# Keys kept by blocks of 128, residue by residue, in a one-core hybrid decoder layer

## The chip, the cores and the metric

The program runs on one core of a Trainium2 chip. The metric is the device time of one execution in microseconds (us).

## The reference

One layer of a decoder trunk, for a prompt of 2048 tokens and for 8 decode rows. Of its four branches two matter here, both banded attention over k and v that the layer's own projection makes. Branch B has 6 heads of 64 and mixes three dilations:

```python
DIL_CONFIGS = ((128, 1), (512, 4), (2048, 16))
def _fold(a, d):          # tokens of one residue mod d become a row of their own
    n, l, h, dh = a.shape
    return a.reshape(n, l // d, d, h, dh).transpose(0, 2, 1, 3, 4).reshape(n * d, l // d, h, dh)
for window, d in DIL_CONFIGS:
    o, lse = _band_attention(_fold(q, d)[:, :, :, None], _fold(k, d), _fold(v, d), slopes[:, None], d)
```

In `_band_attention` each block of 128 queries sees its own 128 keys and the 128 before them, with a bias of -slope * distance. At dilation 16 a residue has exactly 128 tokens, so its only block has no keys before it. Branch D is the same with window 128 for 4 query heads on 2 key heads. The outputs contain k and v themselves and, for the decode rows, their projections.

## The kernel before

Every product of the projection and the scores is made of a high and a low part in fp32r (h_hi, h_lo, w_hi, w_lo; q_both holds q's high part on partitions 0 to 63 and its low part on 64 to 127, k_both holds k's parts twice, once on each half). The program has four stages. First x is normalised and turned. Then the projection walks over 30 column tiles of 128; tiles 21 to 24 are k, 25 to 29 are q. Each tile has five groups of up to 416 tokens in PSUM banks 0 to 4; ScalarE writes main_hi, VectorE writes main_lo, SyncE (SP) stores both to qk_dram, and the decode rows' eight columns go to zs_t. Then comes attention, and last the output stage, which mixes, gates and projects 16 tiles of tokens.

Attention has 176 units in eleven phases of 16. A unit is a block of 128 queries of a pair of heads. The phases are, for head pairs 0 and 1: dilation 1, dilation 16, dilation 4, window branch; for pair 2: dilation 1, 16, 4. Unit n of the first phase is block n; units 16 to 31 are the 16 residues; units 32 to 47 go residue by residue within blocks 0 to 3; unit 64 begins pair 1. In unit n (step s of a loop written out in full) TensorE computes the scores (`scores`, four matmuls with q as weights and 256 key columns moving: for two heads, k high and k low), turns the probabilities of unit s-3 (`turn_probs`), weights v for unit s-5 (`weigh_values`) and, every fourth step, turns the outputs of four units (`turn_out`). VectorE adds the bias table and takes the minimum (logits, L1730), and copies probs_t out of PSUM. ScalarE makes exp (L1352) and copies the outputs; GpSimd gathers the q columns of a residue into q_ring (L906), ahead of its unit, and issues the stores of the outputs (mix, L889). A unit is full when it has keys before its own; the others turn and weight half as much. Keys of a residue are read by a strided view of k_both; a unit of dilation 16 computes the scores of two residues and uses one:

```python
def view(self, t):
    return t[:, 0:T].rearrange("p (t r) -> p r t", r=self.d)
```

k and q come in four pieces of 512 tokens per pair (`load_piece`: k, q and v; then `load_wide` and `load_middle` for v at dilations 16 and 4, `load_swa` for the window branch), all issued by SP in the order of its program. Among these stand the stores of the sample rows (zn, tail_rows, zc_s) and the decode loads (dec_loaded). GpSimd waits for dec_loaded at mix group 4 (step 31) before it loads the first cached decode keys (dec_k), and VectorE computes decode logits from them at steps 36, 38, 46 and 50 of each of the first two pairs. Between the projection and unit 0 TensorE turns the sample rows of 19 tiles and the last rows of two states, and VectorE copies them to zn and tail_rows and computes the bias tables (`pair_tables`).

## Time and profile before

| | |
|---|---|
| median of 3 runs | 1440.78 us (1440.49 to 1443.8) |
| profiled execution | 1441.03 us, span 1439.4 us |
| TensorE matmul busy | 1347.3 us, 94% of the span |
| VectorE, ScalarE, GpSimd busy | 714.3, 461.0, 215.5 us |
| DMA moved | 206.23 MB, mean 143 GB/s |
| mean granted clock | 0.976 |

The table is of the slowest (only) core. Busy TensorE means that a matmul is in flight, not that the array works at its peak. Times in the rows below count from the first instruction. Attention lies between 788 and 1178 us.

### The profile page before, as it was taken

What the parts mean: (1) busy time and instruction counts of PE and PEld (TensorE: products, weight loads), DVE (VectorE), ACT (ScalarE), POOL (GpSimd) and SP (SyncE); (2) the same over time, 40 slices, a digit from 0 to 9 for tenths busy, and PEclk for the clock granted to TensorE, in tenths of its full rate; (3) what the DMA queues carried; (4) which work ended last, traced back from release to release, by engine and by line L of the source; (5) the groups of instructions that cost most, each with busy time, mean ns of one, the idle gap of its engine ahead of it and who ended that gap; (6) DMA issues with size and microseconds to landing.
All of it is one profiled execution on the core that took longest, in us unless ns stands there. A gap on an engine that the chain in (4) does not pass through costs nothing.

```text
span 1439.4 us, 21367 instructions
## 1 busy us (share of the span) xinstructions
PE 1347.3 (94%) x7749; PEld 1167.2 (81%) x7749; DVE 714.3 (50%) x1835; ACT 461.0 (32%) x1189; POOL 215.5 (15%) x264
## 2 busy tenths in 40 slices
PE   5869999999999999999999899999889988999896
PEld 2369999999999999999999676777667647877784
DVE  3592122100335454222121658866789447888783
ACT  5440000121111011222111465666558532343431
POOL 0060000000121211000000053125104310111111
PEclk9989999999999999999999899999999998999998
DMA  8524122121353534444335999945935364555531
GB/s 305 210 87 146 44 87 75 56 87 44 117 184 125 176 103 142 131 140 153 98 117 148 247 261 236 219 105 133 231 87 160 99 208 131 158 177 167 164 125 45
DMA packets 132886, 206.23 MB, mean 143 GB/s; under 512 B 13155, under 2 KB 84484, under 8 KB 130605
## 3 DMA queue, kind: packets, MB, share of 16 engines
q1 hardware_dynamic: 119654, 160.12, 37.7%
q0 software_dynamic: 13152, 45.09, 9.7%
q8 instruction: 45, 0.74, 0.2%
q14 instruction: 35, 0.29, 0.1%
HBM read 136.34 MB, written 68.96 MB: 143 GB/s over the span
## 4 chain that ended last, share of the span: by engine, by line
PE 68%; issue 14%; DVE 7%; DMA 5%; ACT 3%; POOL 2%; SPq 2%; POOLq 0%; DVEq 0%; ACTq 0%
PE psum L973 15%; PE psum L974 15%; PE psum L975 15%; PE psum L1079 4%; PE psum L1106 4%; PE psum L1080 3%; PE psum L1090 3%; PE psum L944 2%; DMA dil_v_p<-kv_nat 2%; PE psum L1115 2%; DMA dec_k<-dil_kc 1%; POOL resid L920 1%; DVE h_f L1470 1%; PE psum L1148 1%; DVE logits L1730 1%
## 5 line engine op out<-in xcount | busy, mean ns | idle before, releaser
L973 PE MATMUL psum<-h_hi,w_hi 128*128 128x416 f32 (+1 forms) x1200 | 422.4, 352 | 12.6 <-POOL h_lo L838 12.6
L974 PE MATMUL psum<-h_lo,w_hi 128*128 128x416 f32 (+1 forms) x1200 | 420.2, 350 | 0.0
L975 PE MATMUL psum<-h_hi,w_lo 128*128 128x416 f32 (+1 forms) x1200 | 419.0, 349 | 0.0
L973 PEld LDWEIGHTS psum<-h_hi,w_hi 128*128 128x128 f32 x1200 | 226.2, 188 | 17.9 <-issue 14.8
L974 PEld LDWEIGHTS psum<-h_lo,w_hi 128*128 128x128 f32 x1200 | 226.2, 189 | 1.4
L975 PEld LDWEIGHTS psum<-h_hi,w_lo 128*128 128x128 f32 x1200 | 226.0, 188 | 1.3
L1352 ACT ACTIVATE probs<-logits,stats 128x256 f32<-128x256 f32 (+1 forms) x352 | 162.2, 462 | 150.2 <-DVE stats L1730 143.9
L1730 DVE CUSTOM_DVE_ANT_0 logits<-psum,bias_dil 128x256 f32<-128x256 f32 (+1 forms) x288 | 93.7, 362 | 83.6 <-PE psum L1080 73.2
L973 PE MATMUL psum<-wo_hi,y_hi 128*128 128x512 f32 x288 | 116.9, 406 | 11.0 <-DVE y_lo L1799 10.8
L975 PE MATMUL psum<-wo_hi,y_lo 128*128 128x512 f32 x288 | 114.3, 397 | 0.0
L974 PE MATMUL psum<-wo_lo,y_hi 128*128 128x512 f32 x288 | 113.9, 396 | 0.0
L1090 PE MATMUL psum<-consts,probs 128*128 128x128 f32 x574 | 97.0, 284 | 11.8 <-DVE probs_t L1716 9.7
L1559 DVE SCALAR_TENSOR_TENSOR main_lo<-psum,main_hi 128x416 fp32r<-128x416 f32 (+1 forms) x45 | 26.3, 584 | 164.5 <-ACT main_hi L1304 164.5
L1552 DVE COPY main<-psum 128x416 f32<-128x416 f32 (+1 forms) x60 | 34.2, 582 | 145.4 <-PE psum L975 145.4
L1256 ACT CAST w_hi<-w_raw 128x1024 fp32r<-128x1024 f32 x30 | 31.3, 1043 | 197.2 <-PE psum L975 174.9
L1090 PEld LDWEIGHTS psum<-consts,probs 128*128 128x128 f32 x574 | 75.4, 150 | 23.3 <-issue 14.9
L1716 DVE COPY probs_t<-psum 128x512 f32<-128x512 f32 x111 | 76.5, 689 | 17.9 <-PE psum L1106 17.1
L1079 PE MATMUL psum<-k_both,q_ring 128*128 128x256 f32 x192 | 84.6, 441 | 0.0
L1106 PE MATMUL psum<-probs_t,v_dil 128*64 128x128 f32 x900 | 83.2, 294 | 0.0
L1080 PE MATMUL psum<-k_both,q_ring 128*128 128x256 f32 x192 | 78.7, 410 | 0.0
L1301 ACT ACTIVATE main<-psum 128x416 f32<-128x416 f32 (+1 forms) x45 | 23.1, 512 | 171.3 <-PE psum L975 171.3
L973 PEld LDWEIGHTS psum<-wo_hi,y_hi 128*128 128x128 f32 x288 | 55.2, 192 | 25.8 <-issue 12.8
(249 smaller groups left out, 1769.0 us busy)
## 6 DMA issues: line engine op xcount, KB each, us to landing
w_raw<-w_tiles POOLq DMA_DIRECT2D x30, 512.0 KB, 6.7
k_both<-qk_dram SPq DMA_DIRECT2D x24, 512.0 KB, 12.5
q_both<-qk_dram SPq DMA_DIRECT2D x40, 256.0 KB, 9.7
mix_dram<-o_st POOLq DMA_DIRECT2D x36, 264.0 KB, 6.0
mix_in<-mix_dram SPq DMA_DIRECT2D x16, 594.0 KB, 4.0
gate_dram<-main SPq DMA_DIRECT2D x9, 1024.0 KB, 3.9
qk_dram<-main_hi SPq DMA_DIRECT2D x9, 1024.0 KB, 4.3
qk_dram<-main_lo SPq DMA_DIRECT2D x9, 1024.0 KB, 7.7
```

Source lines behind the costliest of these rows:

```text
L973: pe.matmul(out, hi, mhi, start=start, stop=False)
L974: pe.matmul(out, hi, mlo, start=False, stop=False)
L975: return pe.matmul(out, lo, mhi, start=False, stop=stop)
L1079: pe.matmul(out, u.q(h), u.keys(0, h), start=True, stop=False)
L1080: m = pe.matmul(out, u.q(h), u.keys(1, h), start=False, stop=True)
L1090: m = pe.transpose(psum[:, PT_BANK + n % 2, P * k:P * k + P], probs[n % 4][:, h, c:c + P], ident)
L1106: m = pe.matmul(psum[64 * h:64 * h + 64, OT_BANK + g % 2, P * (n % 4):P * (n % 4) + P], u.v(h, back), probs_t[n % 2][:, k, :], start=(x == ...
L1256: nc.scalar.copy(w_hi[b][:], w_raw[b][:]).then_inc(w_hi_ready, 1)
L1352: m = nc.scalar.activation(probs[s % 4][:, h, u.cols()], xs_[s % 2][:, h, u.cols()], ACT.Exp, scale=-1.0, bias=st[:, s % 4, 2 * h:2 * h + ...
L1552: last = dve.tensor_copy(main[b][:, c0:c0 + n], bank(g, n))
L1716: dve.tensor_copy(dst[:], src).then_inc(pt_copied, 1)
L1730: m = dve.tensor_tensor_reduce(out=xs_[s % 2][:, h, c], in0=psum[:, S_BANK + s % 2, 256 * h + c.start:256 * h + c.stop], in1=u.bias(h), sc ...
```

## The change

k's tiles are written to main_hi and main_lo in another order of the 2048 columns: in each block of 128 tokens, first the 32 tokens of residue 0 (mod 4), then those of residues 1, 2 and 3. The evacuation of a group of 416 is cut at block bounds for it, 11 pieces a tile instead of 5, and VectorE's operation is a subtraction. In this order a residue of dilation 4 is 32 adjacent columns in each block, a residue of dilation 16 is 8 columns at a stride of 4 columns in each block. A unit of dilation 16 reads its own 128 keys alone. v of dilation 1 and of the window branch is loaded in the same order (four transfers, one for each residue, of 32 partitions each), and the bias tables of dilation 1 and the window branch are permuted.

The transfers of q and k go to 128 partitions: q one head at a time, k one part and head at a time, read twice from DRAM by a broadcast. They were made for 64 partitions at a time. A piece has 10 transfers instead of 5, a window load 20 instead of 17.

The sample rows are turned between units, in steps 2, 5, 7, 9, 11 and 13 on TensorE and one step later on VectorE, in PSUM bank 7. The first bias tables are computed during the last projection tile, ahead of its fourth group. The first window load stands ahead of the sample rows' stores on SP.

```diff
-            for half in range(2):
-                rows = slice(64 * half, 64 * half + 64)
-                eng.dma_start(q_both[kind][rows, :, cols].bitcast(F32),
-                              qk_dram[qt, j, half].rearrange("h r t -> r h t")).then_inc(done, 16)
-                eng.dma_start(k_both[kind][rows, :, cols].bitcast(F32), k.rearrange("a h r t -> r (a h) t")).then_inc(done, 16)
+            for h in range(2):
+                eng.dma_start(q_both[kind][:, h, cols].bitcast(F32), qk_dram[qt, j, :, h]).then_inc(done, 16)
+            for a in range(2):
+                for h in range(1 if kind else 2):
+                    k = qk_dram[3, j, a, p] if kind else qk_dram[p, j, a, h]
+                    eng.dma_start(k_both[kind][:, a if kind else 2 * a + h, cols].bitcast(F32),
+                                  k.unsqueeze(0).broadcast_to([2, 64, 512])).then_inc(done, 16)
+        def load_v(eng, dst, v, done):
+            for r in range(4):
+                eng.dma_start(dst[32 * r:32 * r + 32], v.rearrange("(b j r) c -> r j b c", j=32, r=4)[r]).then_inc(done, 16)
...
-        PIECE_DMAS, SWA_DMAS = 5, 17
+        PIECE_DMAS, SWA_DMAS = 10, 20
...
-                self.own = P if self.full or (d == 16 and self.r % 2) else 0
+                self.own = P if self.full else 0
             def keys(self, part, h):
-                v = self.view(k_both[self.kind][:, part if self.kind else 2 * part + h, :])
+                t = k_both[self.kind][:, part if self.kind else 2 * part + h, 0:T]
                 if self.d == 16:
-                    r0 = self.r - self.r % 2
-                    return v[:, r0:r0 + 2, :]
-                c0 = P * (self.b - 1) if self.full else 0
-                return v[:, self.r, c0:c0 + 256]
+                    return t.rearrange("p (x s i a) -> p s a x i", x=16, s=4, a=4)[:, self.r % 4, self.r // 4]
+                b0 = self.b - 1 if self.full else 0
+                if self.d == 4:
+                    return t.rearrange("p (x s i) -> p s x i", x=16, s=4)[:, self.r, 4 * b0:4 * b0 + 8]
+                return t[:, P * b0:P * b0 + 256]
...
+            load_swa(sp, 0, 0)
             sp.wait_ge(zs_copied, 6)
             sp.wait_ge(zc_ready, 1)
...
-            load_swa(sp, 0, 0)
...
+            def new_rows(s):
+                if s == 2:
+                    pe.wait_ge(nat_copied, len(TURNS))
+                    pe.wait_ge(tail_copied, 1)
...
+                if s in NEW_STEPS:
+                    x = 4 * NEW_STEPS.index(s)
+                    pe.wait_ge(zs_copied, x // 4 + 1)
+                    for y, t in enumerate(ZN_TILES[x:x + 4]):
+                        m = pe.transpose(psum[0:NS, DEC_BANK, P * y:P * y + P], zs_t[:, t, :], ident)
+                    m.then_inc(zs_t_done, 1)
...
-                    out = psum[:, S_BANK + n % 2, 256 * h:256 * h + 256]
+                    out = psum[:, S_BANK + n % 2, 256 * h:256 * h + (P if u.d == 16 else 256)]
...
+                        for a, z in key_parts(c0, c0 + n):
+                            m = nc.scalar.activation(in_keys(main_hi[b], a, z), in_tokens(bank(g), a - c0, z - c0), ACT.Copy,
+                                                     scale=1.0)
...
+                    if ts == NT - 1 and g == 3:
+                        opening()
```

On TensorE, behind the last projection matmul (the branch row ends the projection's loop), the program before has the sample rows (tail_u, tail_z, zs_t) and then the scores of units 0, 1 and on:

```order
L1044 COMPARE_AND_BRANCH
L1051 MATMUL psum<-consts,tail_u 15x128
L1052 MATMUL psum<-consts,tail_z 2x128
L1051 MATMUL psum<-consts,tail_u 15x128
L1052 MATMUL psum<-consts,tail_z 2x128
L1061 MATMUL psum<-consts,zs_t 8x128 x19
L1079 MATMUL psum<-k_both,q_both 128x256
L1080 MATMUL psum<-k_both,q_both 128x256
```

The changed program has at the same place the scores of units 0 and 1 (eight matmuls, of which the last four stand here), and then the tails:

```order
L1100 MATMUL psum<-k_both,q_both 128x256
L1101 MATMUL psum<-k_both,q_both 128x256
L1100 MATMUL psum<-k_both,q_both 128x256
L1101 MATMUL psum<-k_both,q_both 128x256
L1076 MATMUL psum<-consts,tail_u 15x128
L1077 MATMUL psum<-consts,tail_z 2x128
L1076 MATMUL psum<-consts,tail_u 15x128
L1077 MATMUL psum<-consts,tail_z 2x128
```

The 23 small transposes moved behind the first units; the zs_t ones come four at a time in steps 5 to 13.

On SP, from the fourth piece of pair 0 on, the program before has (v_dil are the v tiles, zs_dram is the first of 11 sample-row stores):

```order
L430 DMA q_both<-qk_dram 64x2x512
L432 DMA k_both<-qk_dram 64x4x512
L430 DMA q_both<-qk_dram 64x2x512
L432 DMA k_both<-qk_dram 64x4x512
L436 DMA v_dil<-dil_v_p 128x4x128
L441 DMA v_dil<-dil_v_p 128x16x128
L445 DMA v_dil<-dil_v_p 128x4x128 x4
L724 DMA zs_dram<-zn 8x2432
```

The changed program has from the same piece on (of the four q and k rows of the window load the first two stand here, then its v):

```order
L428 DMA q_both<-qk_dram 128x1x512 x2
L432 DMA k_both<-qk_dram 128x1x512 x4
L438 DMA v_dil<-dil_v_p 32x4x128 x4
L445 DMA v_dil<-dil_v_p 128x16x128
L449 DMA v_dil<-dil_v_p 128x4x128 x4
L428 DMA q_both<-qk_dram 128x1x512 x2
L432 DMA k_both<-qk_dram 128x1x512 x2
...
L438 DMA v_swa<-swa_v_dram 32x16x64 x4
L746 DMA zs_dram<-zn 8x2432
```

The piece has ten rows for five, and 20 window transfers now stand between the v loads and the sample-row stores, the decode loads behind them.

## Rows read from the trace of the kernel before

**Rows 1.** Stretches: length, busy us of PE, PEld, DVE, ACT, POOL, clock, DMA share, GB/s.

```profile
4.00:36.00 32.00, 18.57 (x79) 10.54 (x80) 11.59 (x20) 17.00 (x31) 0.00 (x0) 0.95 0.92 326
...
788.00:828.00 40.00, 32.03 (x234) 25.41 (x233) 26.60 (x94) 19.44 (x67) 3.25 (x5) 0.83 1.00 242
...
828.00:858.00 30.00, 30.00 (x204) 23.11 (x204) 16.12 (x81) 18.52 (x77) 14.36 (x23) 1.00 1.04 261
...
858.00:893.00 35.00, 32.52 (x223) 24.05 (x221) 26.61 (x86) 19.67 (x75) 16.05 (x25) 1.00 0.99 240
...
924.00:954.00 30.00, 28.90 (x274) 23.18 (x270) 24.55 (x90) 21.08 (x76) 5.41 (x8) 1.00 0.86 195
...
1092.00:1122.00 30.00, 30.00 (x208) 23.09 (x206) 24.23 (x96) 23.27 (x85) 13.15 (x20) 1.00 0.45 137
...
1122.00:1178.00 56.00, 56.00 (x347) 35.43 (x346) 23.88 (x96) 23.53 (x85) 11.92 (x18) 1.00 0.43 134
```

**Rows 2.** TensorE in order of time: a full dilation-1 unit and the next one's start.

```profile
946.80 0.39 PE L1079 MATMUL psum<-k_both,q_both 128*128 128x256 f32 x1
...
947.38 0.60 PE L1090 MATMUL psum<-consts,probs 128*128 128x128 f32 x4
...
948.51 0.39 PE L1079 MATMUL psum<-k_both,q_both 128*128 128x256 f32 x1
```

**Rows 3.** TensorE: a dilation-16 unit and the next one's start.

```profile
971.44 0.47 PE L1079 MATMUL psum<-k_both,q_ring 128*128 128x256 f32 x1
...
972.39 0.40 PE L1090 MATMUL psum<-consts,probs 128*128 128x128 f32 x2
...
973.09 0.47 PE L1079 MATMUL psum<-k_both,q_ring 128*128 128x256 f32 x1
```

**Rows 4.** TensorE: a full dilation-4 unit and the next one's start.

```profile
885.03 0.48 PE L1079 MATMUL psum<-k_both,q_ring 128*128 128x256 f32 x1
...
886.03 0.62 PE L1090 MATMUL psum<-consts,probs 128*128 128x128 f32 x4
...
887.17 0.48 PE L1079 MATMUL psum<-k_both,q_ring 128*128 128x256 f32 x1
```

**Rows 5.** VectorE in order of time: decode logits inside a dilation-4 phase.

```profile
864.87 1.35 DVE L1623 TENSOR_TENSOR dec_prod<-dec_k,dec_q 128x1152 f32<-128x1152 f32 x1
...
866.26 1.35 DVE L1626 TENSOR_REDUCE dec_red<-dec_prod 128x18 f32<-128x1152 f32 x1
```

**Rows 6.** Weight loads by form: busy us, mean ns of one.

```profile
L1079 PEld LDWEIGHTS psum<-k_both,q_both 128*128 128x128 f32 x160 | 32.1, 201 | 18.0 <-issue 8.9 <-DVE stats L1730 5.4 <-DMA v_dil<-dil_v_p 3.6
...
L973 PEld LDWEIGHTS psum<-wo_hi,ys_hi 128*8 128x8 f32 x18 | 1.6, 88 | 2.4
```

**Rows 7.** TensorE at the start of attention; 827.77 is unit 16.

```profile
788.32 0.34 PE L975 MATMUL psum<-h_hi,w_lo 128*128 128x392 f32 x1
...
797.41 0.58 PE L1079 MATMUL psum<-k_both,q_both 128*128 128x256 f32 x1 [3.33 <-DVE stats L1730]
...
817.85 0.58 PE L1079 MATMUL psum<-k_both,q_both 128*128 128x256 f32 x1 [3.33 <-DMA v_dil<-dil_v_p]
...
827.77 0.47 PE L1079 MATMUL psum<-k_both,q_ring 128*128 128x256 f32 x1
```

**Rows 8.** VectorE between the projection and unit 0's logits.

```profile
790.54 3.18 DVE L1577 COPY zn<-psum 8x512 f32<-8x512 f32 x5 [0.69 <-PE psum L1061]
...
794.42 0.41 DVE L1582 TENSOR_TENSOR zc_s<-zn 8x256 f32<-8x256 f32 x1
```

**Rows 9.** SP's transfers in order of time.

```profile
775.39 0.69 SPq L430 DMA_DIRECT2D q_both<-qk_dram  x1
...
807.49 12.69 SPq L445 DMA_DIRECT2D v_dil<-dil_v_p  x4
...
826.88 0.40 SPq L734 DMA_DIRECT2D dec_q<-zs_dram  x1
```

**Rows 10.** GpSimd at the first decode-key transfers.

```profile
853.58 1.63 POOL L898 DMA_DIRECT2D dec_k<-dil_kc  x3
```

More of the change, by code:

```diff
@@ L613, in bank, with key_parts, in_keys, in_tokens @@
             return psum[:, b, 0:n]
+        def key_parts(a, z):
+            cuts = [a] + [c for c in (-(-a // P) * P, z // P * P) if a < c < z] + [z]
+            return list(zip(cuts, cuts[1:]))
+        def in_keys(t, a, z):
+            x = a // P
+            if z - a < P:
+                return t[:, P * x:P * x + P].rearrange("p (s i) -> p i s", s=4)[:, (a - P * x) // 4:(z - P * x) // 4]
+            return t[:, a:z].rearrange("p (x s i) -> p x i s", s=4, i=32)
+        def in_tokens(ps, a, z):
+            if z - a < P:
+                return ps[:, a:z].rearrange("p (i s) -> p i s", s=4)
+            return ps[:, a:z].rearrange("p (x i s) -> p x i s", s=4, i=32)
         @block.sync
@@ L1046, in _ @@
                     project(2 * i + b, b, Q0 + 1)
[L1049 to L1062 removed]
+            def new_rows(s):
+                if s == 2:
+                    pe.wait_ge(nat_copied, len(TURNS))
+                    pe.wait_ge(tail_copied, 1)
+                    for m in range(2):
+                        pe.transpose(psum[0:15, DEC_BANK, P * m:P * m + P], tail_u[:, m, :], ident)
+                        last = pe.transpose(psum[0:2, DEC_BANK, 256 + P * m:256 + P * m + P], tail_z[:, m, :], ident)
+                    last.then_inc(tail_t, 1)
+                if s in NEW_STEPS:
[4 more added lines that the diff above has]
+                    m.then_inc(zs_t_done, 1)
             for g in range(4):
@@ L1155, in _ @@
                 decode(s - LAST)
+                new_rows(s)
                 if s < UNITS:
@@ L1523, in chunk, with pair_tables, opening @@
                 last.then_inc(yac_ready, 1)
+            def pair_tables(i, kind):
+                off = consts[:, C_OFF:C_OFF + 256]
+                by_key = lambda z: z.rearrange("p (x i s) -> p x s i", x=2, s=4)
+                blocks = lambda z: z.rearrange("p (x s i) -> p x s i", x=2, s=4)
+                for h in range(2):
+                    if kind and h == 0:
+                        dve.wait_ge(lo_stored[1], 16 * 5)
+                    if kind == 0:
+                        slope = consts[:, bass.ds(C_SLD + 2 * i + h, 1)]
+                        for c, d in enumerate(DILATIONS):
+                            src, dst = (by_key(off), blocks(bias_dil[:, c, h, :])) if d == 1 else (off, bias_dil[:, c, h, :])
+                            last = dve.tensor_scalar(dst, src, slope, float(d), ALU.mult, ALU.mult)
+                    else:
+                        slope = consts[:, bass.ds(C_SLS + 2 * i + h, 1)]
+                        last = dve.tensor_scalar(blocks(bias_swa[:, h, :]), by_key(off), slope, None, ALU.mult)
+                if kind:
+                    last = dve.tensor_copy(sink_now[:], neg_sink[:, bass.ds(2 * i, 2)])
+                last.then_inc(bias_ready, 1)
+                dve.wait_ge(bias_ready, 2 * i + kind + 1)
+            def opening():
+                dve.wait_ge(lo_stored[0], 16 * 4)
+                dve.wait_ge(kv_t, len(TURNS))
+                dve.tensor_scalar(neg_sink[:], neg_sink[:], -1.0, None, ALU.mult).then_inc(sink_negated, 1)
+                dve.wait_ge(sink_negated, 1)
+                pair_tables(0, 0)
             def gate_rows():
@@ L1558, in evac @@
                         dve.wait_ge(act_evac, V0 - GATE0 + 5 * (ts - K0) + g + 1)
-                        last = dve.scalar_tensor_tensor(main_lo[b][:, c0:c0 + n], bank(g, n),
-                                                        -0.125 if kind == "q" else 1.0,
-                                                        main_hi[b][:, c0:c0 + n].bitcast(F32), ALU.mult, ALU.subtract)
+                        if kind == "q":
+                            last = dve.scalar_tensor_tensor(main_lo[b][:, c0:c0 + n], bank(g, n), -0.125,
+                                                            main_hi[b][:, c0:c0 + n].bitcast(F32), ALU.mult, ALU.subtract)
+                        else:
+                            for a, z in key_parts(c0, c0 + n):
+                                dve.tensor_tensor(in_keys(main_lo[b], a, z), in_tokens(bank(g), a - c0, z - c0),
+                                                  in_keys(main_hi[b], a, z).bitcast(F32), ALU.subtract)
                         if kind == "k":
@@ L1721, in _ @@
                     g = s // 4
-                    if u.i == 0 and (u.kind or units[s - 1].kind or s == 0):
+                    if s and u.i == 0 and (u.kind or units[s - 1].kind):
                         pair_tables(u.p, u.kind)
```

73 lines of the change are left out of this document (21 added, 52 removed).

## The prediction

> **What bounds the kernel now.** I read the busy time by stretches first. Attention runs from 788 to 1178 us, in eleven phases of 16 units (a unit: 128 queries of a head pair). In the stride-16 phases TensorE is busy throughout, 30.00 of 30 us, while VectorE has 16.12 and ScalarE 18.52; in the last stride-4 phase it has 56.00 of 56 [rows 1]. So there the end is set by TensorE. In the dense phases (stride 1) and the first two stride-4 phases VectorE is close behind, 24.55 of 30 and 26.61 of 35 us.
>
> Then I read the order of time on TensorE for one full unit of each kind. The four score matmuls (L1079, L1080), counted from the first one's start to the transposes' start, take 0.58 us in a dense unit [rows 2], 0.95 us at stride 16 [rows 3] and 1.00 us at stride 4 [rows 4]. All have 256 moving columns. Only the stride of the moving k differs: 4, 64 and 16 bytes. A whole dense unit takes 1.71 us, a stride-4 unit of the same shape 2.14, a stride-16 unit (half the transposes and weightings) 1.65. The projection ahead (to 788 us) and the output stage (1178 to 1439) do not touch these operands.
>
> **Stride 4 (48 units).** The keys of a residue are now runs of 32 adjacent floats, eight runs to 256 columns, so I price the four matmuls as dense: 2.14 - 1.71 = 0.43 us a unit, 6.9 us a phase. Bounds: nothing gained (stays 1.00 us) to 0.43. I take 0.43, since a run is nearest to the dense form. In the last pair TensorE has no idle time, so 6.9 us stand. In pairs 0 and 1 VectorE computes decode logits inside the phase: a product and a reduction of 1.35 us each, 2.7 us at a time [rows 5], three times a phase (the fourth lies in the window phase behind). Behind each block stand VectorE's copies and logits, for which TensorE waits. Today TensorE is the slower one (VectorE works 26.61 of 35 us there) and part of a block vanishes; 28 us would leave VectorE almost none, as in the dense phase. I charge 0.9 us more a block, so 6.9 - 2.7 = 4.2 us in each. Stride 4 gives 6.9 + 4.2 + 4.2 = 15.3 us.
>
> **Stride 16 (48 units).** 128 columns (own residue only) at 16 bytes replace 256 at 64 bytes. If a strided column costs what it costs now, half of them stream as long as 256 dense ones. The weight load may floor it: 128 columns of q load in 201 ns, 8 columns in 88 [rows 6], so some 113 ns go with the columns, under the 0.145 us that a dense matmul takes (0.58 for four). Both say four in 0.58 us, so 0.95 - 0.58 = 0.37 us a unit, 5.9 a phase. No row has such a matmul under 256 columns: the upper bound is no gain, the lower end 0.45 us a unit with the load hidden further. I take 0.37. Cover: VectorE and ScalarE need 16.12 and 18.52 us for the phase [rows 1], under 30 - 5.9 = 24.1. In pair 2 they have 24.23 and 23.27, so VectorE becomes the bound near 26.5 and 3.5 us remain. Sum: 5.9 + 5.9 + 3.5 = 15.3 us.
> The Trainium skill (SBUF — State Buffer, "Door 1: The DMA port swizzle") says that consecutive reads in a 16-byte line run at full rate and each crossing to a new line pays. The 1.00 and 0.95 us against 0.58 agree; by it stride 16's 128 columns still pay for every column, as I priced them.
>
> **The start.** The last projection matmul starts at 788.32, unit 2 only at 797.41, after 3.33 us of waiting for VectorE [rows 7]. VectorE turned sample rows out meanwhile, 3.18 us in five copies, then tails, product and bias tables [rows 8]. The tables now lie in a gap of the last projection, where VectorE waits for groups; the rest goes between units. Unit 2 can start when VectorE has evacuated the last group and done one unit's logits, about 790.5: 7 us earlier. Given back: 23 small transposes (2.9 us of TensorE) and some 4.4 us of VectorE (the 3.18 and three operations of 0.4) now sit in a dense phase where both are nearly full; I charge 3.5 us. Unit 12 waits 3.33 us for the fourth piece and then runs at half clock (0.83 granted over the stretch [rows 1]; both waits are followed by slow units). In that stretch the DMA engines are full at 242 GB/s; in 828 to 858 us a share of 1.04 moves 261. In the opening of the program, with loads on 128 partitions, a share of 0.92 moves 326, that is 354 when full. q and k loads on 128 partitions should come near that, the fourth piece by about 808, ahead of unit 12 (some 812). That wait and the slow units after it are worth 7 us. 7 - 3.5 + 7 = 10.5: unit 16 moves from 827.77 [rows 7] to 817.3.
> The Trainium skill (same page and section) says partitions 0 to 63 reach only 8 of 16 ports. The full share at 242 to 261 GB/s agrees in direction. By the same rule v, now in four transfers of 32 partitions, gets slower, at most twice: v is 256 of a piece's 1792 KB, so by it a piece would still come sooner. It speaks against the v part alone and changes no term.
>
> **Waits added.** SP issues about 0.64 us per transfer (five end 3.3 us after 775.39 [rows 9]). A piece now has ten (6.4 us), the window k and q with v 20 (12.8 us), and the latter stand ahead of the sample-row stores. Pieces 0 to 2 end at 794.6, stores and piece 3 at 802, the wide and middle v at 805 if the queue is not held as in the 12.69 us row, window loads at 818, the stores take 6.7 us (today from the end of the 12.69 us row to 826.88), then the decode loads carry 1536 + 1024 + 512 KB, 13 us at 240 GB/s: landed about 840, or 849 if the queue holds. I take 843. GpSimd needs them at mix group 4, ahead of the decode-key transfers (853.58 today, nobody held [rows 10]); behind these 1.63 us stand the q gathers of unit 32. The gather is then ready at 845.2; TensorE could be there at 817.3 + 30 - 5.9 = 841.4 (857.8 today). Cost 4 us.
>
> Costed at nothing: k's evacuation in 11 parts instead of 5 (ScalarE and VectorE wait for groups in every projection tile; some 1 us a tile each) and permuted tables. If that cover failed, 1 us x 4 tiles.
>
> **Sum.** 15.3 + 15.3 + 10.5 - 4 = 37.1 us. The profiled execution took 1441.03 us (span 1439.4), the median is 1440.78: 1404 us.
>
> **Rivals.** (A) The 128-column matmuls stay at 0.24 us apiece. Loss 5.9 + 3.5, and in pair 0 only some 2.1 (unit 32 at 847.3 instead of 845.2), as the wait for the decode loads goes: 37.1 - 11.5 = 25.6, 1415 us. For: no such form in the trace; against: weight load and stream both fit 0.145. 0.15. (B) Transfers don't quicken. The decode loads, 840 today, stand behind the window loads, 16 of 256 KB and v, 4.7 MB or 19 us at 245 GB/s, and land at 859: unit 32 starts at 861.3 against 857.8, so the part up to it gives -3.5 instead of +12.4 (10.5 + 5.9 - 4): 37.1 - 15.9 = 21.2, 1420 us. For: the opening's loads have other row lengths. 0.10. (C) VectorE and ScalarE bind more than charged, half of the strided gain of 30.6 gone: 37.1 - 15.3 = 21.8, 1419 us. For: in pair 0's first stride-4 stretch VectorE works 26.61 of 35 us. 0.12. (D) Slower than before: duplicated k rows and 32-partition v make the loads slower than now. In 788 to 893 us the DMA share is 0.99 to 1.04 [rows 1], so no slack covers it there. The pieces and window loads of pairs 0 and 1 are 2 x (7.3 + 4.7) = 24 MB, 98 us at 245 GB/s; at 1.5 times that, 49 us of waits come on top: 1441.0 - 37.1 + 49 = 1453 us. It decides from about 1.4 times. Against: the bytes are the same, and 326 GB/s in the opening. 0.03. (E) Within 0.3% (4.3 us, about what a measurement of this kernel can tell from no change): A, B and C together, 0.02. The forecast itself has 0.58, between 1395 and 1411.
>
> Range: 1392 to 1422. The low end is no GpSimd wait (4 us), full cover in pair 2 (2.4) and blocks that cost nothing more (5.4); the high end takes in A, B and C and leaves out D and E.
>
> **What would show it.** The four score matmuls take about 0.58 us in both strided kinds; stride-4 units 1.71, stride-16 units 1.28 us apart. Unit 2 at 790.5, no wait at unit 12, unit 16 near 817. A GpSimd gap ahead of the first decode-key transfers near 840. Higher GB/s at the same DMA share. I am wrong if those of stride 16 stay at 0.95, or if waits for VectorE or DMA take up the difference.

## The result and the profile after

The changed kernel takes 1792.35 us median of 4 runs (1788.64 to 1794.25), the kernel before 1440.63 us on the same chip: ratio 1.2435, 95% interval 1.2406 to 1.2464. It is 352 us slower, where 1404 us was forecast. The span is 1787.0 us and the mean granted clock 0.875 (before 0.976).

The page of the changed kernel, the chain of work that ended last by engine, and part of the costliest groups (busy us, mean ns | idle us before them and its releasers):

```profile
PE 45%; SPq 31%; issue 12%; DVE 5%; DMA 3%; ACT 2%; POOL 1%; POOLq 0%; DVEq 0%; ACTq 0%
...
L1100 PE MATMUL psum<-k_both,q_both 128*128 128x256 f32 x160 | 59.0, 384 | 254.9 <-DMA v_dil<-dil_v_p 219.5
...
L1100 PE MATMUL psum<-k_both,q_ring 128*128 128x128 f32 (+1 forms) x192 | 61.0, 343 | 80.4 <-POOL q_ring L927 80.4
```

TensorE stands 254.9 us ahead of dense and window units (7.6 in the kernel before) and 80.4 us ahead of one strided unit: together 328 of the 352 us. The second of these is one wait, at unit 32, and the queries' copies there stand behind GpSimd's wait for the decode loads (sink_col, 80.8 us). SyncE, which issues transfers, is on the chain for 31% of the span. SP in order of time, and then stretches of the same kernel (columns as in [rows 1]):

```profile
772.79 1.18 SPq L428 DMA_DIRECT2D q_both<-qk_dram  x2
774.02 19.36 SPq L432 DMA_DIRECT2D k_both<-qk_dram  x4
793.41 6.96 SPq L438 DMA_DIRECT2D v_dil<-dil_v_p  x4
800.41 4.44 SPq L428 DMA_DIRECT2D q_both<-qk_dram  x2
```

```profile
775.00:793.00 18.00, 11.05 (x60) 10.66 (x58) 3.75 (x11) 2.81 (x4) 0.00 (x0) 0.93 0.13 50
838.00:857.00 19.00, 8.74 (x60) 7.09 (x60) 6.71 (x22) 4.37 (x16) 0.00 (x0) 0.68 0.13 50
```

Four transfers of k take SyncE 19.36 us, some 4.8 each, where a transfer of q took 0.69 before [rows 9], and meanwhile the DMA engines have a share of 0.13 and move 50 GB/s, where [rows 1] has 240 to 261 GB/s at a share of about 1. The share is that of two busy engines of sixteen. The start and length of each DMA packet in the trace say the same: from 775 to 793 us two packets are in flight for 15.5 of the 18 us and hardly ever more than three, where the kernel before has 16 or more in flight for 26.7 of the 30 us from 828 to 858. So most DMA engines have no work. The pieces then land one by one, and TensorE waits 22.2 us at unit 0 and then again at units 4, 8 and 12 of the first phase (TensorE in order of time; the wait in brackets):

```profile
840.50 0.58 PE L1100 MATMUL psum<-k_both,q_both 128*128 128x256 f32 x1 [27.19 <-DMA v_dil<-dil_v_p]
...
872.50 0.58 PE L1100 MATMUL psum<-k_both,q_both 128*128 128x256 f32 x1 [23.26 <-DMA v_dil<-dil_v_p]
...
911.07 0.58 PE L1100 MATMUL psum<-k_both,q_both 128*128 128x256 f32 x1 [29.12 <-DMA v_dil<-dil_v_p]
```

In [rows 7] the only such wait, for a piece, was 3.33 us.

The matmuls themselves did what was forecast. The changed kernel's four score matmuls of a stride-4 unit, at the full granted clock, and the transposes behind them:

```profile
1484.09 0.39 PE L1100 MATMUL psum<-k_both,q_ring 128*128 128x256 f32 x1
1484.31 0.28 PE L1101 MATMUL psum<-k_both,q_ring 128*128 128x256 f32 x1
1484.43 0.28 PE L1100 MATMUL psum<-k_both,q_ring 128*128 128x256 f32 x1
1484.55 0.28 PE L1101 MATMUL psum<-k_both,q_ring 128*128 128x256 f32 x1
1484.67 0.38 PE L1111 MATMUL psum<-consts,probs 128*128 128x128 f32 x2
```

They take 0.58 us from the first one's start to the transposes' start, 1.00 before [rows 4]. Each phase has 16 units; the lengths below are from the first score matmul of one unit to that of another, by TensorE's rows in order of time, in us. A column is one execution, the traced one: for e9 it is the slowest of its six (1432.02 us), for e12b, e16 and e17 the fastest (1395.49, 1412.32 and 1406.94), so a few us between two columns can be those of the execution.

| units, kind | before | after | e1 | e9 | e10 | e11 | e12a | e12b | e16 | e17 |
|---|---|---|---|---|---|---|---|---|---|---|
| 0 to 16, dense | 34.9 | 112.7 | 39.2 | 37.9 | 35.7 | 33.1 | 33.6 | 35.6 | 34.7 | 35.5 |
| 16 to 32, stride 16 | 29.8 | 104.6 | 40.6 | 24.2 | 24.2 | 24.2 | 29.8 | 24.2 | 25.0 | 24.2 |
| 32 to 48, stride 4 | 35.4 | 34.1 | 37.9 | 40.5 | 38.1 | 41.0 | 32.7 | 26.6 | 33.0 | 30.7 |
| 48 to 64, window | 31.4 | 31.7 | 31.2 | 31.1 | 34.1 | 30.8 | 29.2 | 29.4 | 30.9 | 30.9 |
| 80 to 96, stride 16 | 29.8 | 24.2 | 24.2 | 24.2 | 24.2 | 24.2 | 29.8 | 24.2 | 24.2 | 24.2 |
| 96 to 112, stride 4 | 36.4 | 68.5 | 36.2 | 35.4 | 35.6 | 36.5 | 32.7 | 26.6 | 30.8 | 30.5 |
| 112 to 128, window | 33.0 | 37.9 | 31.8 | 30.7 | 31.9 | 31.6 | 29.2 | 29.7 | 30.9 | 31.3 |
| 144 to 160, stride 16 | 30.3 | 31.8 | 32.4 | 34.5 | 27.1 | 27.1 | 30.3 | 27.2 | 26.9 | 26.7 |
| 160 to 174, stride 4 | 41.2 | 35.8 | 35.9 | 37.4 | 35.7 | 41.2 | 41.2 | 35.5 | 35.5 | 35.5 |

In the changed kernel an undisturbed stride-16 phase is 5.6 us shorter and the last stride-4 stretch 5.4. Two questions follow: what makes the transfers slow, and how much of the forecast 37 us is there without that.

### The profile page after: what moved, and what is told of

It is laid out like the page before. It is cut to its first block, busy times and chain, and to the rows that moved or that the text cites. A ratio compares the mean times of both kernels' runs of the same rounds, so it can differ in the third digit from the quotient of the medians.

```text
span 1787.0 us, 21483 instructions
## 1 busy us (share of the span) xinstructions
PE 1334.2 (75%) x7749; PEld 1158.4 (65%) x7749; DVE 723.4 (40%) x1859; ACT 468.6 (26%) x1213; POOL 219.5 (12%) x264
## 3 DMA queue, kind: packets, MB, share of 16 engines
q1 hardware_dynamic: 119254, 160.12, 26.7%
## 4 chain that ended last, share of the span: by engine, by line
PE 45%; SPq 31%; issue 12%; DVE 5%; DMA 3%; ACT 2%; POOL 1%; POOLq 0%; DVEq 0%; ACTq 0%
SPq L432 17%; PE psum L994 12%; PE psum L995 12%; PE psum L996 12%; SPq L428 6%; SPq L438 5%; PE psum L965 2%; SPq L449 1%; PE psum L1127 1%; POOL resid L941 1%; DVE h_f L1496 1%; PE psum L1100 1%; PE psum L1111 1%; PE psum L1169 1%; DMA dil_v_p<-kv_nat 1%
## 5 line engine op out<-in xcount | busy, mean ns | idle before, releaser
L1100 PE MATMUL psum<-k_both,q_both 128*128 128x256 f32 x160 | 59.0, 384 | 254.9 <-DMA v_dil<-dil_v_p 219.5
L1100 PEld LDWEIGHTS psum<-k_both,q_both 128*128 128x128 f32 x160 | 36.9, 230 | 267.1 <-DMA v_dil<-dil_v_p 199.5
L994 PE MATMUL psum<-wo_hi,y_hi 128*128 128x512 f32 x288 | 116.9, 406 | 11.6 <-DVE y_lo L1841 11.4
L1100 PE MATMUL psum<-k_both,q_ring 128*128 128x128 f32 (+1 forms) x192 | 61.0, 343 | 80.4 <-POOL q_ring L927 80.4
L1111 PE MATMUL psum<-consts,probs 128*128 128x128 f32 x574 | 104.8, 301 | 10.4 <-DVE probs_t L1760 5.1
L1100 PEld LDWEIGHTS psum<-k_both,q_ring 128*128 128x128 f32 x192 | 38.8, 202 | 93.6 <-POOL q_ring L927 82.0
L1127 PE MATMUL psum<-probs_t,v_dil 128*64 128x128 f32 x900 | 88.0, 307 | 0.0
L1278 ACT CAST w_hi<-w_raw 128x1024 fp32r<-128x1024 f32 x30 | 31.4, 1048 | 197.3 <-PE psum L996 175.0
L910 POOL DMA_DIRECT2D mix_dram<-o_st x36 | 26.8, 743 | 432.5 <-ACT o_st L1362 428.7
```

What stands on the lines that cost most here:

```text
L994: pe.matmul(out, hi, mhi, start=start, stop=False)
L1100: pe.matmul(out, u.q(h), u.keys(0, h), start=True, stop=False)
L1111: m = pe.transpose(psum[:, PT_BANK + n % 2, P * k:P * k + P], probs[n % 4][:, h, c:c + P], ident)
L1127: m = pe.matmul(psum[64 * h:64 * h + 64, OT_BANK + g % 2, P * (n % 4):P * (n % 4) + P], u.v(h, back), probs_t[n % 2][:, k, :], start=(x == ...
```

## The experiments

Ratios are to the kernel before on the same chip, each with its 95% interval; "one run" has none.

**e1_qk_halves, e3_only_loads, e7_q_two_k_halves: which part of the change makes it slow.** e1 is the changed kernel with the q and k transfers of before (two halves of 64 partitions; v still by residue):

```diff
-            for h in range(2):
-                eng.dma_start(q_both[kind][:, h, cols].bitcast(F32), qk_dram[qt, j, :, h]).then_inc(done, 16)
-            for a in range(2): ... k.unsqueeze(0).broadcast_to([2, 64, 512])
+            for half in range(2):
+                rows = slice(64 * half, 64 * half + 64)
+                ... qk_dram[qt, j, half].rearrange("h r t -> r h t")
+                ... k.rearrange("a h r t -> r (a h) t")
```

e3 is the kernel before with nothing but the changed q and k transfers. e7 is the changed kernel with q as changed (its outermost dimension is 2, but nothing is read twice) and k in halves.

> The changed kernel with q and k transfers as before the change (two halves of 64 partitions, rows outermost); v by residue, key order, own keys and turned rows stay. Theory S (the source's slowest dimension has size 2 and confines a q or k transfer to 2 of 16 DMA engines: DMA share 0.13 and 50 GB/s while they stand alone): the 350 us go, SP issues take about 0.6 us again and the time is 1400 to 1420 us; the first piece stretch runs at a DMA share near 1 and over 200 GB/s. Rival R (the v transfers of 32 partitions, or SP's longer order of work, hold the loads): time stays above 1600 us. Rival K (the reads of permuted k by TensorE or the permuted evacuation slow something): stays well above 1441.

> The kernel before with nothing but the q and k transfers of the changed one (7 transfers a piece, 17 a window load). Theory S: 1750 to 1800 us, units 4, 8 and 12 of each pair wait 20 to 35 us, DMA share 0.13 meanwhile, SP held some 5 us by each k transfer. Rivals R and K: close to 1441.

> The changed kernel, q in two transfers with an outermost dimension of 2 and no broadcast, k as before the change. Theory S says that q alone, 512 KB a piece and 2 engines, takes 10 us a piece at 50 GB/s where it stands alone: between 1430 and 1560 us, with stretches at a share of 0.13. Rival B (the zero-stride read of k from DRAM is what is slow, not the outermost 2): q runs at full share and the time is that of the version with halves, 1400 to 1420.

Measured: e1 1439.79 us (ratio 0.9999, 0.9979 to 1.0020), e3 1780.94 us (one run), e7 1556.8 us (one run). The transfers alone make 340 us of the 352, with every other part as before, and undoing them alone removes it all. Reading k twice is not the cause: q is 40 of the 104 changed transfers, is read once, and costs 117 us over e1. The stretch of e7 in which SyncE issues two transfers of q (787.57 to 792.53 us) has much the same low share and rate (there too two packets are in flight, for 3.6 of the first 4.5 us):

```profile
788.00:793.00 5.00, 0.58 (x4) 0.25 (x2) 0.63 (x2) 1.77 (x2) 0.00 (x0) 1.00 0.17 54
```

What q and k have in common is the outermost dimension of size 2 in the access pattern (for q the two halves a, for k the broadcast), in place of 64 in the kernel before. But e1 is not faster than the kernel before, where 1400 to 1420 us was expected: 37 us of gain are missing.

**e8_128_spread: 128 partitions with all DMA engines.** q and k stand in DRAM so that one transfer's outermost dimension is 128 rows, for which k is stored twice:

```diff
+        k_dram = scratch("k_dram", [4, 4, 2, 2, 2, 64, 512])
+                    eng.dma_start(k_both[...], k.rearrange("x r t -> (x r) t")).then_inc(done, 16)
```

> The changed kernel, q and k loaded to 128 partitions from a source whose slowest dimension is 128: q's parts stand next to each other in DRAM, k is stored twice (8 stores of 64 partitions a k tile instead of 2, 4 a q tile), and nothing is broadcast. Theory S: 16 engines and both halves of the partitions, a 256 KB transfer lands 0.7 us after the one before, not 1.2; over 300 GB/s at full share; 1395 to 1410 us, 5 to 15 us under the version with halves. If the port halves of SBUF do not matter, it equals the version with halves or is some us slower for its doubled stores.

Measured: 1443.53 us, ratio 1.0015 (1.0000 to 1.0029). No gain, so the number was missed, but the trace tells two things. A stretch of the first units of e8, and SP in order of time in e8's k tiles:

```profile
812.00:838.00 26.00, 23.82 (x221) 19.32 (x220) 21.77 (x79) 17.80 (x67) 3.26 (x5) 1.00 1.08 332
```

```profile
604.11 5.79 SPq L728 DMA_DIRECT2D k_dram<-main_hi  x4
609.94 9.88 SPq L728 DMA_DIRECT2D k_dram<-main_lo  x4
```

At a full share this stretch of pieces, v loads and stores of q moves 332 GB/s, where the kernel before has 240 to 261 [rows 1]. From the last projection matmul (809.44) to unit 16 (837.27) e8 takes 27.8 us, where the kernel before takes 39.45 [rows 7]: 11.6 us less, about the 10.5 that the prediction expected of the start. So its reasoning on 128 partitions was sound, given an outermost dimension that lets all DMA engines in. But the high and low stores of a k tile (four transfers each, for two heads and two copies) hold SyncE 15.7 us, and the projections end some 21 us later than before (809.44 against 788.32). e8 also has the wait at unit 32 that e9 below removes, 11.6 us here. The price was moved ahead, not saved.

**e9_window_last: the wait at unit 32.** Comparing e1 with the kernel before, unit by unit (table), the largest loss is at 16 to 32: 40.6 us. e1 on SP, and then GpSimd and TensorE at unit 32:

```profile
816.17 1.34 SPq L430 DMA_DIRECT2D q_both<-qk_dram  x1
...
827.32 10.10 SPq L437 DMA_DIRECT2D v_swa<-swa_v_dram  x4
837.52 3.28 SPq L745 DMA_DIRECT2D zs_dram<-zn  x1
...
856.53 0.33 SPq L766 DMA_DIRECT2D sink_col<-sink_rows  x1
```

```profile
861.83 1.63 POOL L918 DMA_DIRECT2D dec_k<-dil_kc  x3 [16.76 <-DMA sink_col<-sink_rows]
```

```profile
864.14 0.58 PE L1099 MATMUL psum<-k_both,q_ring 128*128 128x256 f32 x1 [16.35 <-POOL q_ring L926]
```

The window stage's 20 transfers hold SyncE from 816.17 to 837.5 us, the sample rows' stores and decode loads stand behind them, GpSimd waits 16.76 us for the last of these, and its query copies for unit 32 stand behind that wait. e9 puts them back:

```diff
-            load_swa(sp, 0, 0)
             sp.wait_ge(zs_copied, 6)
...
             sp.dma_start(sink_col[:], sink_rows).then_inc(dec_loaded, 16)
+            load_swa(sp, 0, 0)
```

> The kernel of e1_qk_halves with one move undone: SyncE issues the 20 transfers of the first window stage (q, k, v) behind the sample rows' stores and decode loads, where the kernel before has its 17, not ahead of them. In e1 these 20 transfers took SyncE from 816.2 to 837.5 us, so the first store of the sample rows went at 837.5 (before: 820.5), the last decode load at 856.5 (before: 835.8), and GpSimd waited 16.8 us for it, so unit 32 started at 864.1, 19.7 us behind unit 30. Theory L (the gain is real, and this one move gave it back): that wait is gone, the two steps from unit 30 to unit 32 take about 3.5 us, all that follows stands some 16 us earlier, and the time is 1421 to 1427 us. Rival E (something behind the attention units sets the end, so that earlier units do not end the kernel earlier): unit 32 starts 16 us earlier, and the time stays at 1435 to 1441. Rival W (the window stage's loads are late next, at unit 48): 1430 to 1435, with a wait for v_swa or the window's q there.

Measured: 1423.49 us, ratio 0.9882 (0.9864 to 0.9901), inside the expected 1421 to 1427; 16 to 32 takes 24.2 us.

**e10_rows_first, e14_q_on_128: the start.** e10 is e9 with the sample rows turned ahead of unit 0, so it is the kernel before plus the order of k, own keys at stride 16, and v by residue. e14 is e9 with q on 128 partitions, its outermost dimension 128, k in halves:

```diff
-                eng.dma_start(q_both[kind][rows, :, cols]..., qk_dram[qt, j, half].rearrange("h r t -> r h t"))
+                eng.dma_start(q_both[kind][:, half, cols]..., q_dram[qt - 4, j, half].rearrange("a r t -> (a r) t"))
```

> The kernel of e9_window_last with the sample rows turned before unit 0 again, on TensorE and VectorE as in the kernel before; so it is the kernel before with nothing but k kept by residue, stride 16 with own keys only, and v loaded by residue. It prices the move of the rows. Theory L: in e1 unit 0 began 8.5 us earlier than before but unit 16 only 4.2 us (the loads of the pieces were late instead), so this kernel is 4 to 6 us slower than e9_window_last, 1425 to 1431 us, which leaves 10 to 15 us below the kernel before for the cheaper matmuls. Rival: if the move of the rows is what gains and the matmuls are not, 1436 to 1441.

> The kernel of e9_window_last with q alone stored so that one transfer fills 128 partitions (its outermost dimension 128), k still in two halves of 64 partitions. In e8_128_spread, where both stood so, a q transfer took 5.0 us from issue to landing (9.7 before), but storing k twice cost SyncE 15.7 us for a tile instead of 0.9 and the projections ended 20 us later. Here only q is stored in four transfers for a tile instead of two. Theory P (the start is bound by the pieces' landing; width of the transfer buys some of it): unit 16 begins 2 to 4 us earlier after the last projection than in e9 (38.1 us): 1419 to 1422. Rival: bytes bind, not ports: the same as e9_window_last within 1 us, or slower where the stores of q delay the last projections.

Measured: e10 1423.88 us, ratio 0.9886 (0.9867 to 0.9905), not told apart from e9, where 4 to 6 us more were expected, so no gain from the move of the rows is seen. e14 1429.93 us, ratio 0.9928 (0.9905 to 0.9951), some 0.5% slower than e9, where 1419 to 1422 us was expected. In e9 the last projection matmul starts at 788.90 and unit 0 directly behind it, at 789.1 (before: 4.6 us behind). But unit 16 is at 826.99, 38.1 us behind the last projection, against 39.45 before [rows 7] and 38.0 in e14 (789.03, 827.05). That 1.4 us is no gain either: e11 and e12a, which start as the kernel before does, take 37.7 and 38.2 us for it. The stretch 790 to 818 us of the kernel before, of e9 and of e14:

```profile
790.00:818.00 28.00, 20.83 (x158) 16.65 (x156) 20.76 (x72) 14.24 (x52) 0.76 (x1) 0.86 1.09 259
```

```profile
790.00:818.00 28.00, 19.00 (x152) 15.12 (x149) 17.43 (x65) 14.92 (x52) 0.76 (x1) 0.88 1.09 258
```

```profile
790.00:818.00 28.00, 19.28 (x153) 15.30 (x151) 17.62 (x65) 15.04 (x52) 0.76 (x1) 0.88 1.09 258
```

The DMA engines are full and equally fast in all three. TensorE begins earlier and waits longer for the same bytes (e9: 8.7 us for v_dil in two waits; 3.33 before). Widening q alone (e14) buys none of what e8 shows for q and k together.

**e11_own_keys_only: columns or contiguity at stride 16.** One edit in the kernel before:

```diff
-                    r0 = self.r - self.r % 2
-                    return v[:, r0:r0 + 2, :]
+                    return v[:, self.r, :]
```

> The kernel before with one edit: stride 16 takes its 128 own keys alone, in a 128-column matmul that still reads k 64 bytes apart. It tells columns from contiguity. If a matmul's time goes by its columns alone (about 0.12 us for 128), the 16 units of stride 16 take about 24.2 us in a pair as in e1 (29.8 before), 5 us less in two of three pairs: 1427 to 1433 us. If reading keys 64 bytes apart is what costs (0.24 us stays for 128 columns), nothing moves: 1438 to 1443. In between if the surcharge is per column.

Measured: 1434.99 us, ratio 0.9957 (0.9936 to 0.9977), somewhat less gain than the expected 1427 to 1433; one execution of twelve, at 2543.89 us, stands apart from all others. TensorE in order of time, e11, 128 columns read 64 bytes apart:

```profile
958.34 0.36 PE L1078 MATMUL psum<-k_both,q_ring 128*128 128x128 f32 x1
958.52 0.29 PE L1079 MATMUL psum<-k_both,q_ring 128*128 128x128 f32 x1
958.63 0.29 PE L1078 MATMUL psum<-k_both,q_ring 128*128 128x128 f32 x1
958.75 0.29 PE L1079 MATMUL psum<-k_both,q_ring 128*128 128x128 f32 x1
958.86 0.40 PE L1089 MATMUL psum<-consts,probs 128*128 128x128 f32 x2
```

Four matmuls in 0.52 us, 0.95 before [rows 3]; the keys 16 bytes apart of e9 and e10 give the same phase, 24.2 us. At stride 16 the new order of k bought nothing, the halved columns everything. The table shows one more thing. e11's stride-4 matmuls are those of the kernel before, yet phase 32 to 48 takes 41.0 us against 35.4: what units 16 to 32 gained is lost there, where VectorE waits 0.97 and 3.45 us for dec_k at the row steps (0.90 at one of them before).

**e13_third_row_later, e15_rows_apart: other places for the row steps.** Edits of one line in e9: ROW_STEPS (36, 38, 48, 50), and (36, 41, 48, 54), in place of (36, 38, 46, 50).

> The kernel of e9_window_last with the third row step of each pair at step 48 instead of 46, so that VectorE does not stand still for the dec_k load that GpSimd issues three units before (e1: 3.87 us at unit 110, 1.88 before; TensorE waited 4.8 us there, and units 110 to 112 took 9.7 us against 6.8). Theory L: the stride-4 phases' gain went into that wait, so two pairs give 2 to 3 us each, 4 to 6 us together: 1416 to 1422. Rival: VectorE is the bound there anyway and the work only moves: the same as e9_window_last within 1.5 us.

> The kernel of e9_window_last with the four row steps of a pair at 36, 41, 48 and 54 instead of 36, 38, 46 and 50: none waits for its load, and no two of them are close. e13_third_row_later showed that the wait at unit 48 goes (7.2 us earlier there) but only 3.4 us are left at unit 64. Theory V: it is VectorE's work in the window, spread here further: 1 to 3 us less than e9_window_last, 1419 to 1423. Rival: the window units behind it have no room either: 1422 to 1425.

Measured: e13 1422.42 us, ratio 0.9890 (0.9864 to 0.9916); e15 1427.31 us, ratio 0.9922 (0.9905 to 0.9939). 1416 to 1422 and 1419 to 1423 us were expected; neither is shown to be faster than e9, so moving the steps gained nothing that the runs can tell. In e13 the phase 32 to 48 falls from 40.5 to 33.0 us and the window phase behind it rises from 31.1 to 34.9.

**e12a_before_no_rows, e12b_keys_no_rows: without the row steps.** Both leave out the loads of dec_k and all but 36 of the 1152 columns of each row step's product and sum, so the sample rows' logits are not computed; e12a from the kernel before, e12b from e10.

```diff
-                dve.wait_ge(dec_k_loaded[x % 2], 48 * (2 * i + x // 2 + 1))
-                dve.tensor_tensor(prod, dec_k[x % 2][:], dec_q[...].broadcast_to([P, 3, 384]), ALU.mult)
+                dve.tensor_scalar(prod, dec_q[:, bass.ds(n, 1), 0:36]..., 1.0, None, ALU.mult)
```

> The kernel before without the eight row steps of the sample rows: the loads of dec_k are left out, and of each step's product and sum (1152 columns, 2 x 1.35 us on VectorE) 36 columns remain, so the sample rows' logits are not computed. It is the base for e12b_keys_no_rows. The steps stand in the stride-4 phases of two pairs, where units 32 to 48 took 35.4 us and units 96 to 112 took 36.4; the third pair has none, and there 12 units of full stride 4 took 34.7. Theory V (VectorE's row steps and their loads bind in those phases): 6 to 12 us faster than the kernel before, 1429 to 1435. Rival: they were hidden beside TensorE's slow stride-4 matmuls: 1437 to 1441.

> The same left out of e10_rows_first (the kernel before with k by residue, own keys in stride 16, v by residue). With the row steps, e10 gained 17 us over the kernel before: by the starts of units 5.6 and 5.6 in stride 16, about 4.6 in stride 4 of the third pair (0.38 us for a unit), and next to nothing in stride 4 of the first two (phase 96 to 112: 0.8 us). Theory V: without the row steps stride 4 gains there too, some 5 us in each, so the distance to e12a_before_no_rows is 23 to 28 us, and the time 1403 to 1410. Rival B (something else, the probabilities' copies or ScalarE, binds in stride 4 once TensorE is cheap): the distance stays at 17 us.

Measured: e12a 1429.62 us (0.9933, 0.9919 to 0.9948), e12b 1396.58 us (0.9720, 0.9699 to 0.9741). The distance is 33.0 us by the medians and 31 by the ratios, above the expected 23 to 28, where e10 stands 17.0 us under the kernel before (1440.84 - 1423.88). So the row steps cost the kernel before 10.7 us and e10 27.3 by the medians (10 and 24 by the ratios, whose intervals are 2 to 3 us to each side). By the table 32 of the 33 us are 5.6 + 5.6 + 3.1 at stride 16 and 6.1 + 6.1 + 5.7 at stride 4.

**e16_row_loads_early, e17_work_without_loads, e18_before_row_loads_early: the steps' work or their loads.** In e10 VectorE in order of time at the first step of pair 0, and TensorE behind it:

```profile
858.78 1.36 DVE L1671 TENSOR_TENSOR dec_prod<-dec_k,dec_q 128x1152 f32<-128x1152 f32 x1 [2.09 <-DMA dec_k<-dil_kc]
860.17 1.35 DVE L1674 TENSOR_REDUCE dec_red<-dec_prod 128x18 f32<-128x1152 f32 x1
```

```profile
862.22 0.41 PE L1109 MATMUL psum<-consts,probs 128*128 128x128 f32 x2 [4.00 <-DVE probs_t L1748]
...
863.18 0.58 PE L1098 MATMUL psum<-k_both,q_ring 128*128 128x256 f32 x1
863.56 0.42 PE L1099 MATMUL psum<-k_both,q_ring 128*128 128x256 f32 x1
```

The load was issued at 847.7. TensorE stands 4.00 us and its next score matmuls start 0.21 us apart or more (0.12 at full clock). The granted clock behind that wait is half:

```profile
866.00:870.00 4.00, 2.79 (x15) 2.11 (x13) 3.93 (x12) 0.83 (x3) 0.63 (x1) 0.50 0.91 243
```

e17 is e10 with the full product and sum on dec_q instead of dec_k and no loads. e16 and e18 are e10 and the kernel before with the loads issued four units earlier:

```diff
-        ROW_GROUPS, ROW_STEPS = (4, 5, 7, 8), (36, 38, 46, 50)
+        ROW_GROUPS, ROW_STEPS = (3, 4, 6, 7), (36, 38, 46, 50)
```

> The kernel of e10_rows_first with GpSimd issuing each row step's load of dec_k one group (four units) earlier: behind groups 3, 4, 6 and 7 of a pair instead of 4, 5, 7 and 8. In e10 the load of the first step was issued at 847.7 us and VectorE waited for it 2.1 us until 858.8; TensorE stood 4.0 us behind that step and then ran several units at half clock. Theory L (the late loads take the gain): no wait for dec_k of more than 0.5 us is left, the stretch from unit 32 to 64 and from 96 to 128 shrinks by 4 to 7 us each: 1409 to 1416 us. Theory V (VectorE's work of 2.7 us a step takes it): 1420 to 1424, with the same stalls of TensorE behind DVE probs_t.

> The kernel of e10_rows_first with VectorE's row steps at full size but without their loads: the product takes dec_q instead of dec_k, so the sample rows' logits are not those of the keys. Theory L: work alone costs little, 1397 (e12b_keys_no_rows) plus 3 to 8 us: 1400 to 1406. Theory V: most of the 27 us between e12b and e10 is the work: 1412 to 1422. If it lies between, both share.

> The kernel before with its dec_k loads four units earlier, as a control. Its units are longer (2.14 us against 1.71 at stride 4), and its waits for dec_k were 1.9 and 0.9 us. Theory L: it gains too, but less than e16 does over e10: 3 to 6 us, 1435 to 1438. Theory V: within 0.3% of the kernel before.

Measured: e17 1410.52 us (0.9794, 0.9776 to 0.9813), between the two theories: of the 27.3 us the work alone makes 13.9, the loads 13.4, by medians of runs on three chips that are good to 2 or 3 us. e18 1435.63 us (0.9968, 0.9948 to 0.9987), 5.8 us under the kernel before by the medians: there the earlier loads do help. e16 1421.44 us (0.9873, 0.9852 to 0.9894), four runs from 1412.3 to 1425.9, where e10's six lie from 1419.6 to 1426.1: not told apart by the median. Its profiled execution took 1412.3 us. The stretch 845 to 905 us of e10, e16 and e12b in turn:

```profile
845.00:905.00 60.00, 49.08 (x368) 37.45 (x366) 44.80 (x146) 33.37 (x127) 21.88 (x35) 0.86 1.06 254
```

```profile
845.00:905.00 60.00, 51.38 (x437) 39.43 (x437) 50.01 (x168) 37.93 (x145) 25.06 (x40) 0.97 1.09 254
```

```profile
845.00:905.00 60.00, 57.70 (x517) 45.52 (x518) 49.78 (x190) 45.23 (x169) 16.53 (x25) 1.00 1.09 243
```

The columns to read are TensorE's count and the clock: 368, 437 and 517 matmuls in the same 60 us, at 0.86, 0.97 and 1.00. In e16 no step waits for dec_k, and TensorE's waits behind VectorE's copies in this stretch are at most 1.8 us (4.0 in e10), but they don't vanish. In the traced executions the four phases with row steps take 125.6 us in e16, 139.7 in e10 and 123.4 in e17, so this execution got back nearly all that the loads cost. The other three of e16 (1420.9 to 1425.9 us) did not, and none of them was traced. That late loads cost the 13.4 us is thus seen in one execution and not shown by the medians.

## Why the prediction was wrong

**The step that failed** is in "The start": "q and k loads on 128 partitions should come near that, the fourth piece by about 808". It took 354 GB/s from the opening's loads because both fill 128 partitions, and so read the number of partitions as what sets the rate. The runs showed 50 GB/s, and unit 12, which the fourth piece holds up, at 911.07. e3 and e1 show that the transfers as written cost about 340 us, e7 that it is not the double read, and the share of 0.13 with two packets in flight that two of sixteen engines carried them. e8, with all engines in, shows a start 11.6 us shorter, so the price of the term was right and its condition was missed. With it fell "SP issues about 0.64 us per transfer": 19.36 us for four. The decode loads, forecast to land by 843, had their last issued at 1018, and unit 32 waited 80.4 us. The Trainium skill (DMA: Bandwidth & Descriptors, "Why a DMA increments its semaphore by 16 and not by 1") states the rule: a transfer is split over the largest number of engines, up to 16, that divides the size of the slowest dimension other than 1 of both its patterns. The trace agrees: 2/16 is 0.125, and 0.13 was measured.

**Rival D** had the right place (slower transfers, on the path) but the wrong mechanism and size. It argued from "the bytes are the same" to 0.03; 50 GB/s against 240 to 261 is about five times the transfer time, where D decides from 1.4 times and was priced at 1.5, 49 us. "B (transfers don't quicken)" is about what e9 shows at the start.

**Stride 4** (15.3 us forecast) was right in its gross size: 0.43 us a unit, 6.9 a phase, against 6.1, 6.1 and 5.7 us measured without row steps. "I charge 0.9 us more a block" was the mis-sized term. Three such blocks were to cost 2.7 us a phase; by e12a, e12b and e10 the row steps cost 16.6 us more with cheap matmuls than with dear ones (27.3 against 10.7), over eight steps some 2 us each. About half of the 27.3 us is VectorE's work alone (e17). For the other half the traces show what it left out: the loads of the steps are issued a fixed number of units ahead, so shorter units bring VectorE to them before they land (waits for dec_k of 7.1 us in all in e10, 4.3 before), and TensorE's granted clock was half behind the longest of these stalls. e16 takes these waits away and gains in its traced execution, but not clearly in its median, so this half stays open. In e10 the four phases that hold them (32 to 64, 96 to 128) are together 3.5 us longer than before, and only the last pair's stride 4 gained (5.5). That is rival C, at 0.12. Beyond the 5.4 us charged for two phases the row steps took 11.2 us more (16.6 - 5.4; the fourth step of a pair lies in the window phase), against C's 15.3.

**Stride 16** (5.9 + 5.9 + 3.5 forecast): 5.6 + 5.6 + 3.2 in e10. The four matmuls take 0.52 us where 0.58 was forecast. Right, though e11 shows that only the columns matter. Rival A fell.

**The start** (10.5 us forecast): with the transfers in halves nothing is left of it. The 7 us of earlier start are real at unit 2 (9.1 us behind the last projection matmul before, 2.0 in e9) and lost by unit 16, since the pieces land no sooner. **Waits added** (4 us forecast): 80.4 us in the changed kernel and 16.4 in e1. For e1 the sum had the window loads from 805 to 818, 12.8 us; they ran from 816.2 to 837.5, 21.3 us, 10.10 of them for the window's v. The wide and middle v ahead of them took 13.8 us of SyncE, the case that the sum named and did not take ("if the queue is not held").

Sum of what the parts are worth with the transfers in halves and the window loads behind: 17 us (e9, e10), not 37.1; with the row steps gone, 33.

k's evacuation in 11 parts, costed at nothing, shows no cost: the last projection matmul starts between 784 and 789 us in the runs with it (e8 apart, for its stores), between 785 and 789 in those without.

**Open:** why e9's profiled execution has half clock in phase 144 to 160 and e10's does not. Stretches of e9 and then of e10:

```profile
1092.00:1102.00 10.00, 8.68 (x52) 6.32 (x50) 6.71 (x29) 7.98 (x26) 5.57 (x8) 0.66 0.65 203
1102.00:1112.00 10.00, 10.00 (x50) 6.90 (x49) 7.15 (x31) 4.82 (x20) 3.81 (x6) 0.50 0.17 52
```

```profile
1092.00:1102.00 10.00, 8.27 (x68) 5.88 (x68) 9.18 (x38) 9.14 (x32) 6.39 (x7) 1.00 0.71 227
1102.00:1112.00 10.00, 9.18 (x74) 6.88 (x75) 7.81 (x44) 7.04 (x31) 5.18 (x9) 1.00 0.09 28
```

TensorE was idle about as long in the first stretch of both (1.3 and 1.7 us of 10), yet one was granted 1.2 GHz for the next stretch and the other kept 2.4. It makes phase 144 to 160 34.5 us instead of 27.1, and fits the spread of e9's runs (1420.8 to 1432.0). Whether the 128-column units invite it was not tried. Why three executions of e16 are 9 to 14 us slower than its traced one was not seen. Nor was a way to bring k to 128 partitions without SyncE's 15.7 us a tile.

## What to carry to other kernels

Read a transfer's access pattern for its outermost dimension before its bytes and partitions: a DMA share of 0.13 with SyncE busy for microseconds per transfer was here the sign of a pattern that only two engines carry. When matmuls get cheaper, list the work of other engines that stands between them, and what is issued a fixed number of units ahead, and compare its length and landing time with the new unit time; here the row steps, their work and their loads together, took half of the gain (17 us with them, 33 without). And price a change's parts apart: own keys, k's order and a queue order that stayed as it was made 1.2% (e9, e10), inside a change that lost 24%.

## What the runs showed of the hardware

Transfers whose outermost dimension is 2 moved 50 GB/s at a share of 0.13, with two packets in flight, and those of k held SyncE some 4.8 us each (0.6 to 0.7 for a transfer of the kernel before where the queue was free). At a full share, a stretch in which q and k go to 128 partitions with outermost dimension 128 moved 332 GB/s (e8), one with q and k in halves of 64 partitions 258 (e9); v loads and stores are in both. A 128-column fp32r score matmul starts 0.11 to 0.12 us behind the last (the second of a unit 0.18) whether its keys lie 64 bytes apart (e11) or 16 (e9, e10), where 256 columns 64 or 16 bytes apart take 0.22 to 0.24 (before); 256 columns in runs of 32 floats take 0.12 (after). Behind a wait of TensorE of 4.00 us the granted clock was 0.50 for the next units (e10).
